# A streaming encoder step: attention's transposes and scores in one break, recurrence's scores beside its decay rows

## The reference, cut to what matters

```python
h = rmsnorm(x, g1); z = h @ w_in          # (mq, mk, mv, mo, mi, mf, sb, sc, sx, dq, dk, dv, gt)
# A) mLSTM recurrence, chunkwise; b = cumsum(log forget gate), per head
w = exp(where(causal, b[:, None] - b[None, :] + ig[None, :], -inf) - mt)    # decay rows
s = (q @ k.T) * w
num = s @ v + inter * (q @ C);  den = max(|sum(s) + inter * (q @ n)|, exp(-mt))
hm = num / den;  C = il * C + (wl * k).T @ v;  n = il * n + (wl * k).sum(0)
# B) short convolution: sb * dwconv3(sc * sx)
# C) differential attention, 4 heads, two 64-wide maps per head, 128-wide values
p1, p2 = softmax(q1 @ k1.T), softmax(q2 @ k2.T)     # chunk-causal mask for the prompt
o = rmsnorm((p1 - lam * p2) @ v, da_g)
x = x + sum(sigmoid(gate_b) * (branch_b @ w_branch[b])) @ w_out
# then a ConvFFN: up-projection, causal depthwise convolution, SiLU-gated product, down-projection
```

## Time and profile before

| | |
|---|---|
| median of 3 runs | 991.29 us |
| the profiled execution | 991.47 us, span of its instructions 989.6 us |
| TensorE, matmuls | busy 970.8 us (98%) |
| TensorE, weight loads | busy 949.2 us (96%) |
| VectorE | busy 690.0 us (70%) |
| ScalarE | busy 471.4 us (48%) |
| GpSimd | busy 162.7 us (16%) |
| mean granted clock of TensorE | 0.997 |

### The profile page before, as it was taken

The page is one execution under the profiler, slowest core; times in us unless marked ns, Lnnn a source line. Parts: engine busy times, 40 slices in busy tenths (PEclk is TensorE's granted clock), DMA queues, the critical chain, the costliest instruction groups (busy, mean ns, idle before and its releaser), DMA issues.

```text
span 989.6 us, 20109 instructions
## 1 busy us (share of the span) xinstructions
PE 970.8 (98%) x7751; PEld 949.2 (96%) x7751; DVE 690.0 (70%) x1162; ACT 471.4 (48%) x980; POOL 162.7 (16%) x346
## 2 busy tenths in 40 slices
PE   7999999999999999999999999999999999999996
PEld 6999899999999998999999999999999999999996
DVE  7886666678667899877776547777777777634354
ACT  5675555565565766555553433333333333422242
POOL 2000121110111222121112211111111112111011
PEclk9999999999999999999999999999999999999998
DMA  6522323264331223233244222222222222432252
GB/s 198 197 86 86 96 89 109 76 206 132 90 86 45 85 86 86 65 98 96 77 128 165 85 69 92 84 98 88 85 86 87 85 86 81 130 93 76 84 149 93
DMA packets 104086, 99.87 MB, mean 101 GB/s; under 512 B 4868, under 2 KB 99481, under 8 KB 103735
## 3 DMA queue, kind: packets, MB, share of 16 engines
q1 hardware_dynamic: 98799, 85.51, 28.2%
q10 hardware_dynamic: 4072, 10.23, 3.1%
q0 software_dynamic: 1120, 2.86, 0.8%
HBM read 91.26 MB, written 7.31 MB: 100 GB/s over the span
## 4 chain that ended last, share of the span: by engine, by line
PE 91%; DVE 4%; issue 2%; ACT 2%; DMA 0%; POOL 0%; DVEq 0%; POOLq 0%; ACTq 0%
PE D L1750 51%; PE D L1809 28%; PE D L1769 2%; PE X L2052 1%; PE X L2090 1%; DVE w_l L1329 1%; ACT w_h L1036 1%; PE D L1894 1%; PE D L1781 1%; PE D L1944 1%; PE X L1998 1%; PE X L1999 0%; PE X L1984 0%; DVE tw L1349 0%; PE X L2001 0%
## 5 line engine op out<-in xcount | busy, mean ns | idle before, releaser
L1329 DVE TENSOR_TENSOR w_l<-raw,w_h 128x512 fp32r<-128x512 f32 (+1 forms) x286 | 200.9, 720 | 129.6 <-ACT w_h L1036 127.9
L1809 PE MATMUL D<-a_h,w_h 128*128 128x272 f32 x840 | 249.7, 297 | 1.4 <-DVE tmp L1512 1.0
L1809 PE MATMUL D<-a_h,w_l 128*128 128x272 f32 x840 | 243.0, 289 | 0.0
L1809 PE MATMUL D<-a_l,w_h 128*128 128x272 f32 x840 | 241.6, 288 | 0.0
L1036 ACT ACTIVATE w_h<-raw 128x512 fp32r<-128x512 f32 (+1 forms) x286 | 171.4, 617 | 83.1 <-PE D L1750 72.0
L1809 PEld LDWEIGHTS D<-a_h,w_h 128*128 128x128 f32 x840 | 158.1, 188 | 5.5 <-issue 2.4
L1809 PEld LDWEIGHTS D<-a_l,w_h 128*128 128x128 f32 x840 | 158.4, 189 | 0.0
L1809 PEld LDWEIGHTS D<-a_h,w_l 128*128 128x128 f32 x840 | 157.9, 188 | 0.0
L1750 PE MATMUL D<-h_h,w_h 128*128 128x272 f32 x704 | 145.9, 288 | 0.0
L1750 PE MATMUL D<-h_h,w_l 128*128 128x272 f32 x704 | 145.7, 288 | 0.0
L1750 PE MATMUL D<-h_l,w_h 128*128 128x272 f32 x704 | 145.1, 288 | 0.0
(11 more groups left out here) (362 smaller groups left out, 1670.7 us busy)
## 6 DMA issues: line engine op xcount, KB each, us to landing
raw<-in_w_in SPq DMA_DIRECT2D x64, 512.0 KB, 4.1
raw<-in_w_up SPq DMA_DIRECT2D x44, 512.0 KB, 4.3
raw<-in_w_down SPq DMA_DIRECT2D x20, 512.0 KB, 3.8
raw<-in_w_branch SPq DMA_DIRECT2D x12, 512.0 KB, 3.5
raw<-in_w_out SPq DMA_DIRECT2D x8, 512.0 KB, 4.5
raw<-in_w_down SPq DMA_DIRECT2D x10, 384.0 KB, 3.3
x_spill<-xT ACTq DMA_DIRECT2D x1, 2176.0 KB, 7.4
xT<-x_spill ACTq DMA_DIRECT2D x1, 2176.0 KB, 10.0
```

What stands on the lines that cost most here:

```text
L1329: v.tensor_tensor(split_view(w_l, g), whole_view(g), split_view(w_h, g).bitcast(F32), ALU.subtract)\
L1809: last = t.matmul(out, wt[:, k, :], x[:, left, k, :], start=w in (1, 2, 5) and k == i == 0, stop=k == KQ - 1 and i == 2, skip_group_check= ...
```

## The change

Only due times move; every step keeps its instructions, its waits and its operands.

Recurrence: `s` is due with `lw` (so it follows it in the same break), and `qi` one tick earlier, with `w`. `pt`, `kw`, `n` and all later steps keep theirs.

Attention: with t0, t1 and t2 the due times of the scores of u, u + 1 and u + 2 (the distances between scores of successive steps are 5, 6, 7 and 10 ticks), `t` of u is due at t1, that is just ahead of the scores of u + 1 in the same break; `wt` a tick later; `o` at t1 + 2.5, `sq` and `rr` a tick after it, `on` at t1 + 6, `y` at t2 + 2.5 (beside `o` of u + 1, as before), `yt` and `yc` a tick later. For u = 0 `t` and `o` keep their times, `on` comes 2.5 later.

```diff
-        for dt, sub in ((0, "lw"), (1, "s"), (1, "w"), (2, "qi"), (2, "pt"), (2, "kw"), (4, "n"), (5, "rd"), (6, "sq"),
+        for dt, sub in ((0, "lw"), (0, "s"), (1, "w"), (1, "qi"), (2, "pt"), (2, "kw"), (4, "n"), (5, "rd"), (6, "sq"),
                         (6, "c"), (6, "rr"), (7, "hn"), (8.9, "h"), (10, "hm")):
...
     for u in range(17):
-        t0, t1 = (99 + 28 * (x // 4) + (0, 5, 11, 18)[x % 4] if x >= 0 else 91 for x in (u - 1, u))
-        for dt, sub in ((0, "s"), (1, "mx"), (2, "ex"), (3, "wd"), (5.5, "t"), (6.5, "wt"), (8, "o"), (9, "sq"),
-                        (9, "rr"), (11.5, "on"), (t1 - t0 + 8, "y"), (t1 - t0 + 9, "yt"), (t1 - t0 + 9, "yc")):
-            if u or dt > 2:
-                at_time(t0 + dt, "at", sub, u)
+        t0, t1, t2 = (99 + 28 * (x // 4) + (0, 5, 11, 18)[x % 4] if x >= 0 else 91 for x in (u - 1, u, u + 1))
+        t, o = (t1, t1 + 2.5) if u else (t0 + 5.5, t1)
+        for time, sub in ((t0, "s"), (t0 + 1, "mx"), (t0 + 2, "ex"), (t0 + 3, "wd"), (t, "t"), (t + 1, "wt"), (o, "o"),
+                          (o + 1, "sq"), (o + 1, "rr"), (t1 + 6, "on"), (t2 + 2.5, "y"), (t2 + 3.5, "yt"),
+                          (t2 + 3.5, "yc")):
+            if u or time > t0 + 2:
+                at_time(time, "at", sub, u)
```

## The result

The changed kernel takes 992.99 us (median of 11 runs, 992.36 to 995.59) beside 991.56 us of the kernel before on the same chip: 1.0019 times as long, 95% interval 1.0011 to 1.0028. It is 1.4 us slower; 988.2 us and a gain were forecast, and the range ended at 990.2.

The account below looks back on a forecast made before the run. TensorE was taken as the bound, busy 970.8 of 989.6 us. Recurrence -1.95 and attention -1.0 sum to -2.95; from a median of 991.29 that gives 988.3, and half of 0.2 for sharing 988.2 us; range 985.6 to 990.2.

Parts of the forecast that it names:

- recurrence's waits: Second prompt tile: `qi` a block earlier finishes `p_ml` some 0.7 us earlier, so TensorE's 0.3 us wait at `n` goes.
- the joined break: Recurrence: `s` and `lw` in one break cost 2.59 us instead of 2.90; 0.33 taken per break, 1.65 for five.
- its passages are the same: Recurrence, the stream's narrower tile (32 columns): passages between selector and full-height weights taken to be as in the other tiles.
- sharing in attention: Attention: `t` sharing a break with the next scores saves 0.02 us at most; 0 taken for eleven new pairs.
- Rival 3: Attention: each break has a fixed price of 0.46 us, so eleven fewer give 5.1 us: 984.3 us; chance 0.05.
- the 986.4: Attention: time in us if each break that goes saves the Trainium skill's drain estimate, 0.17 us, 1.8 for eleven.
- Attention's waits: Attention: old waits that go, less new ones and those that stay, give -1.0 us; bounds -4.0 and +1.8.
- step 9: Attention, first query block of a head: `t`, joined to the next scores, waits about 0.7 us for probabilities; bounds 0 and 1.8.
- the bank's wait: Attention: TensorE's 1.0 us wait for a PSUM bank ends at 378.93 whatever TensorE did before; earlier gains are lost there.
- The drains behind it: Attention: a drain ending at 392.37 leaves 0.4 of 1.6 us won; a later weight split takes 0.2.
- Rival 5: Attention: a waiting `t` holds the next scores, 1.8 us in each of four heads, net +5.3: 996.6 us; chance 0.05.
- the clock left out: TensorE: a lower clock in longer breaks was not counted, since the granted clock reads 9 in every slice but the last.

Follow-up runs that it names:

- experiment 4: Kernel before with recurrence's changed times (`s` beside `lw`) but `qi` left at its old time: 994.57 us, ratio 1.0034.
- experiment 3: Kernel before with recurrence's part of the change, and ScalarE's `w` due with `lw` and `s`: 989.94 us, ratio 0.9981.
- experiment 5: Changed kernel with `hm` due half a block later, behind `w` on ScalarE: 989.55 us, ratio 0.9982.
- experiment 7: Kernel before with attention's part of the change, but `t` and `wt` a block after the next scores, not in their break: 991.29 us, ratio 0.9998.
- experiment 9: Changed kernel with `w` also due with `lw` and `s`: 989.31 us, ratio 0.9974.
- experiment 8: Kernel before with `n` grouped, four query matmuls then four probability matmuls, part of the numerators' sum left out: 990.65 us, ratio 0.9989.
- experiment 10: Changed kernel with `w` due with `lw` and `s`, and `n` grouped (part of the sum left out): 988.73 us, ratio 0.9973.
- experiment 11: Changed kernel with `w` due with `lw` and `s`, and `n` reordered with one head's sum open per bank, nothing left out: 988.37 us, ratio 0.9974.
- experiment 2: Kernel before with recurrence's part of the change alone, attention as before: 993.39 us, ratio 1.0019.

## Why the prediction was wrong

**The step that failed** is the one on recurrence's waits: "`p_ml` is done some 0.7 earlier: the 0.3 goes", with its ground, "so it waits for nothing new", and the sum "Recurrence: -1.65 - 0.3 = -1.95". `qi`'s 0.7 is right (experiment 4). But the step followed `qi` on VectorE and kept everything else where it was. `s` had been TensorE's work between the block whose drain opens ScalarE's chain and the `n` at its end; moved ahead of that block, it is still executed, but covers nothing. The forecast counted `s` as cost and not as cover: the old wait, plus the cover lost, less `qi`, is the new wait to the hundredth (0.28 + 1.68 - 0.67 = 1.29). The same was missing for the third tile (0.69) and for the fourth's values (1.09). Recurrence came to +1.7 instead of -1.95, which is 3.65 of the 4.8 us between forecast and result (of the rest, 0.3 is that the kernel before took 991.56 here, 0.3 lies in attention, 0.4 is the clock's). Experiments 3 and 5 show the cause from two sides, by an earlier `w` and by a later `hm`.

**Right: the joined break**, 2.56 us for 2.59; in all -1.5 for -1.65. The sum's own gain was 0.31 a break, and the 0.33 taken for it had no row behind it; 0.34 was measured here. The stream's, the first and the fourth tile's breaks, which transposes of keys or values share, gave less (0.24, 0.28, 0.29): "its passages are the same" holds of the passages, not of what they cost there.

**Right: sharing in attention saves nothing** (experiment 7). Rival 3 falls; its 984.3 also left out the 1.0 us for waits that the 986.4 beside it counts (983.3 with it).

**Attention's waits**: which go and which stay was right; the sum came near by luck. TensorE's timeline in the changed kernel at step 9, at the bank's wait and at the pair of steps 11 and 12:

```profile
362.70 0.29 PE L1811 MATMUL D<-a_h,w_l 128*128 128x272 f32 x1
363.39 0.33 PE L2075 MATMUL X<-ident,prob 128*128 128x128 f32 x1 [0.40 <-DVE prob L1374]
...
364.54 0.29 PE L1811 MATMUL D<-a_l,w_h 128*128 128x272 f32 x1
...
382.86 0.39 PE L1811 MATMUL D<-a_h,w_h 128*128 128x272 f32 x1 [0.98 <-DVE tmp L1514]
...
387.37 0.29 PE L1811 MATMUL D<-a_h,w_l 128*128 128x272 f32 x1
387.50 0.49 PE L2075 MATMUL X<-ident,prob 128*128 128x128 f32 x3
...
389.24 0.29 PE L1811 MATMUL D<-a_l,w_h 128*128 128x272 f32 x1
```

Step 9 waits 0.4 (0.7 forecast), steps 1, 5 and 13 not at all, `wdT` and both late `prob` are gone, the bank's wait is still there: all as written. But it did not end "whatever TensorE did before": counted from the dense matmul ahead of attention's first transposes (245.17 before, 249.77 here) it ends at 133.09 us instead of 133.76, 0.7 earlier, with the same length, so what was won until then was kept and not "lost there". The drains behind it, in turn, came to 1.7 us with their restarts (0.56, 0.76 and 0.78 between starts, less three steps) where 0.6 was forecast. The two errors, 0.7 and 1.1, work against each other: -0.8 by the medians for -1.0 is in part luck. Rival 5, the slower one, looked for the loss in the wrong half of the change: no `t` held the scores by more than 0.4.

**Wrong: the clock left out.** "The granted clock reads 9 in every slice but the last" is true, and says nothing of 4 us in a slice of 25. Windows of the changed kernel (length, busy time and count of PE, PEld, DVE, ACT and POOL, then the granted clock, DMA share and GB/s):

```profile
109.00:114.00 5.00, 5.00 (x34) 3.13 (x33) 3.32 (x6) 1.30 (x3) 0.00 (x0) 1.00 0.01 3
114.00:118.00 4.00, 4.00 (x22) 4.00 (x21) 0.93 (x4) 1.65 (x7) 0.00 (x0) 0.57 0.00 0
...
186.00:193.00 7.00, 6.20 (x37) 5.83 (x37) 2.85 (x6) 1.57 (x3) 0.00 (x0) 0.76 0.48 150
```

In the two stretches at 0.57 and 0.76 dense matmuls are 0.225 us apart for a time (0.125 elsewhere): the lower of the clock's two levels, 1.2 GHz. They cost 1.5 us (from the stream's `n` to the next break, 11.52 us, in experiment 9's trace 10.01) and 1.6 (from the fourth tile's joined break to the next one, 7.32 for 5.73 in experiment 3's). They explain why the profiled execution took 995.5 us; they are not the loss, since executions without them take 992.6 us beside 991.6 of before.

## What to carry to other kernels

A step on the bounding engine has a cost, and it is also cover for every chain that runs on other engines meanwhile. Before moving one, list the chains that start ahead of it and end behind it, and put their slack beside its length. Here the chain had none in the second tile and some 0.3 us in the third, and moving 1.68 us of `s` past its start gave, without `qi`'s gain, 1.68 us more of waiting in the one (0.28 to 1.96, experiment 4) and 1.35 in the other. And then look at the order in the queue of the idle engine: the same change loses 1.4 us or gains 1.9 to 2.3, by the place of one operation on ScalarE.

## What the runs showed of the hardware that was not expected

- Two matmuls in a row whose weights have different heights (128 and 32 rows) cost 0.11 us more than two of one height, at the stream's `n`; the 36-row selector and back, 0.35 us for a passage there and one back at the joined break of the second tile, if the passages are what was saved there (experiment 7 shows that a break as such has no price). In tiles of 128 rows the same alternation costs nothing: grouping left their `n` at 2.68 us.
- The clock can fall behind a break in which TensorE was not idle: in the changed kernel's trace the stretch ahead of 114 us is the stream's `n`, 3.96 us of small matmuls with no wait. With `n` grouped (3.28 us, experiment 8) the mean granted clock was 0.997 or 0.998 in all 11 runs, while 8 of 29 runs of the kernel before beside it show 0.995. But experiments 10 and 11 have a short `n` too, and in each three runs show 0.996 and take some 2 us more; no trace shows where the clock fell in them. Experiment 2's trace has no fall at `n` (3.97 us there) and one at the fourth tile's joined break. So whether the shorter `n` is the reason stays open.
